# Hybrid decoder step on one core: keys and values loaded every second turn, the page chain a slot later, gate products between long chunks, low parts on VectorE

## What is computed

```python
n = rms_norm(x, g_mix)
q, k, v, xr, gr, gates = jnp.split(n @ w_in, SPLITS, axis=-1)
attn = attend(q, k, v, sb_bias)          # stick-breaking weights: exp(log_sigmoid(z) + tail sum of log_sigmoid(-z))
xc, _ = causal_dwconv(xr, rnn_buf, w_rnn_conv, b_rnn_conv)
r = sigmoid(xc @ w_rgate); i = sigmoid(xc @ w_igate)      # block diagonal, 16 blocks of 64
a = exp(-RG_C * r * softplus(-lam)); u = sqrt(1 - a*a) * i * xc
h = scan(a, u); rnn = h * gelu(gr)
gate_a, gate_b = sigmoid(gates)
x = x + (gate_a * attn + gate_b * rnn) @ w_out
```

## Time and profile before

| | us |
|---|---|
| median of 3 runs | 2364.26 |
| lowest and highest run | 2360.05, 2374.73 |
| profiled execution | 2364.8 |
| its span, first to last instruction | 2363.1 |
| TensorE busy (matmul), share of the span | 1972.6, 83% |
| VectorE busy | 1173.9, 50% |
| ScalarE busy | 940.9, 40% |
| GpSimd busy | 327.2, 14% |

### The profile page before, as it was taken

One profiled execution on the slowest core, in us unless ns is written; L12 is line 12 of the kernel. 1 busy time (PEld: TensorE's weight loads), 2 busy tenths in 40 slices (PEclk: granted clock), 3 DMA queues, 4 the chain that ended last, 5 costly groups with the idle time before them and its releaser, 6 DMA issues. The chain is left out here.

```text
span 2363.1 us, 41678 instructions
## 1 busy us (share of the span) xinstructions
PE 1972.6 (83%) x14580; PEld 1789.8 (76%) x14580; DVE 1173.9 (50%) x1987; ACT 940.9 (40%) x1514; POOL 327.2 (14%) x150
## 2 busy tenths in 40 slices
PE   4996967968687696967968779699999999999986
PEld 3896857757576584856757558699999999999985
DVE  6101535537365463635637453355555565455555
ACT  4112546655565665546655631222112222122213
POOL 4121100000000000000000120222112221122210
PEclk9998988979889797988979789799999999999998
DMA  3333222122221213222122222111111111111104
GB/s 116 97 92 84 70 61 63 44 70 59 78 66 39 70 48 79 63 62 64 44 70 59 64 96 86 53 54 42 33 50 44 46 52 36 36 52 45 44 18 159
DMA packets 206432, 148.21 MB, mean 63 GB/s; under 512 B 66485, under 2 KB 194550, under 8 KB 206228
## 3 DMA queue, kind: packets, MB, share of 16 engines
q1 hardware_dynamic: 206254, 145.99, 21.3%
HBM read 128.57 MB, written 17.61 MB: 62 GB/s over the span
## 5 line engine op out<-in xcount | busy, mean ns | idle before, releaser
L87 PE MATMUL d_p_up<-n_hi,d_w_hi 128*128 128x350 f32 x1056 | 343.7, 326 | 14.0 <-POOL d_w_lo L1613 7.7
L87 PE MATMUL d_p_up<-n_lo,d_w_hi 128*128 128x350 f32 x1056 | 342.8, 325 | 0.0
L87 PE MATMUL d_p_up<-n_hi,d_w_lo 128*128 128x350 f32 x1056 | 342.6, 324 | 0.0
L1760 DVE TENSOR_TENSOR mix<-mix,d_p_down 128x350 f32<-128x350 f32 x264 | 137.2, 520 | 320.9 <-PE d_p_down L1807 320.9
L87 PE MATMUL b_p_proj<-n_hi,b_w_hi 128*128 128x350 f32 x768 | 279.9, 364 | 0.0
L1657 ACT ACTIVATE d_up<-d_p_up 128x350 f32<-128x350 f32 x132 | 60.7, 461 | 499.8 <-PE d_p_up L87 499.8
L87 PE MATMUL b_p_proj<-n_lo,b_w_hi 128*128 128x350 f32 x768 | 258.0, 336 | 0.0
L87 PE MATMUL b_p_proj<-n_hi,b_w_lo 128*128 128x350 f32 x768 | 257.0, 335 | 0.0
L918 ACT ACTIVATE b_sums<-b_p_z,b_bias 128x720 f32<-128x720 f32 (+16 forms) x136 | 94.8, 697 | 379.9 <-PE b_p_z L1189 353.4
L1009 DVE COPY mix<-b_p_misc 128x64 f32 (+2 forms) x136 | 29.8, 219 | 420.3 <-PE b_p_misc L1220 417.9
L875 POOL TENSOR_TENSOR b_w_lo<-w_raw,b_w_hi 128x1024 fp32r<-128x1024 f32 x33 | 78.9, 2392 | 1012.2 <-ACT b_w_hi L891 1012.2
(11 more groups left out here) (248 smaller groups left out, 4066.1 us busy)
## 6 DMA issues: line engine op xcount, KB each, us to landing
w_raw<-in_w_in SPq DMA_DIRECT2D x45, 512.0 KB, 4.1
w_raw<-in_w_up SPq DMA_DIRECT2D x45, 512.0 KB, 3.8
b_page<-in_cache_k SPq DMA_DIRECT2D x128, 128.0 KB, 2.1
b_page<-in_cache_v SPq DMA_DIRECT2D x128, 128.0 KB, 2.1
w_raw<-in_w_down SPq DMA_DIRECT2D x22, 512.0 KB, 3.2
b_q_in<-q_scr SPq DMA_DIRECT2D x272, 32.0 KB, 2.3
q_scr<-a_q_stage SPq DMA_DIRECT2D x16, 260.0 KB, 3.3
b_k_in<-k_scr SPq DMA_DIRECT2D x16, 260.0 KB, 3.7
```

What stands on the lines that cost most here:

```text
L87: last = pe.matmul(out, w[:, k, :], x[:, k, col:col + CW], start=(k == 0 and w is w_hi and x is x_hi), stop=(k == KT - 1 and w is w_lo))
L1760: dve.tensor_tensor(to, to, p_down[:, n % 4, 0:CW], ALU.add).then_inc(down_out, 1)
```

## The change

Keys and values are loaded only in the first of two turns that share them; in the other, SP raises the semaphores by what the loads would have added. SP's loop runs over groups with two turns in its body. The first two query loads of a turn and its keys are issued ahead of the last two page loads of the turn before, and the values ahead of slot 3's page load. The key pages are transposed in slots 1 to 8 and multiplied in slots 2 to 9, the steps after them move by a slot, the value pages are multiplied in slots 14 to 16 and in slot 0 of the next turn, and the heads are picked in slot 3. The first gate product is made after the second gr chunk, and after it one stands between each two long chunks. The last step of the convolution moves from slot 11 to slot 9. The low parts are formed by VectorE, behind its transposed weights of the slot, and the fourth weight tile moves from slot 12 to 13.

```diff
-CHUNK_ORDER = [(w, c) for w in ("xr", "ga", "gr") for c in range(CHUNKS)] + \
-    [("rg", 0), ("gb", 0), ("ig", 0), ("rg", 1), ("gb", 1), ("ig", 1), ("rg", 2), ("gb", 2), ("ig", 2)]
+CHUNK_ORDER = [(w, c) for w in ("xr", "ga") for c in range(CHUNKS)] + \
+    [("gr", 0), ("gr", 1), ("rg", 0), ("gr", 2), ("rg", 1), ("gb", 0), ("rg", 2), ("gb", 1), ("ig", 0), ("gb", 2),
+     ("ig", 1), ("ig", 2)]
...
-W_AT = (1, 4, 8, 12)
-V_STEPS = {13: (0, 1), 14: (2, 3), 15: (4, 5), 16: (6, 7)}
-PAGES_AT = {**{s: (s + 2,) for s in range(8)}, 13: (10, 11), 14: (12, 13), 15: (14, 15)}
+W_AT = (1, 4, 8, 13)
+V_STEPS = {14: (0, 1), 15: (2, 3), 16: (4, 5), 17: (6, 7)}
+PAGES_AT = {**{s + 1: (s + 2,) for s in range(8)}, 14: (10, 11), 15: (12, 13)}
...
-                with sp.Fori(0, KT, 1) as i:
-                    group = i // 2
-                    load_q(i, 0)
-                    load_q(i, 1)
-                    load_pages(i, 0)
-                    load_pages(i, 1)
-                    sp.wait_ge(qk_done, nth(i, SLOTS, SLOTS - 1))
...
+                def first_loads(i, group, fresh):
+                    load_q(i, 0)
+                    load_q(i, 1)
+                    if fresh:
+                        sp.wait_ge(qk_done, nth(i, SLOTS, SLOTS - 1))
+                        sp.sem_inc(passed, 1)
+                        load_k(group)
+                    else:
+                        sp.sem_inc(k_arr, 32)
+
+                def turn_loads(i, group, fresh):
                     load_q(i, 2)
                     load_q(i, 3)
                     load_w(1, nth(i, 4, 1), i * P + GA_COL)
                     sp.wait_ge(inits, 6)
+                    load_w(0, nth(i, 4, 2), i * P + GR_COL)
+                    load_pages(i, 0)
+                    load_pages(i, 1)
                     sp.wait_ge(proj_done, nth(i, CHUNK_NS, CHUNK_NS - 1))
...
                     for s in range(SLOTS - 1):
                         if s + Q_RING < SLOTS - 1:
                             load_q(i, s + Q_RING)
                         if s == SLOTS - 3:
                             load_q(i, SLOTS - 1)
+                        if s == LAG and fresh:
+                            sp.wait_ge(av_group, nth(i, GROUPS, GROUPS - 1))
+                            sp.sem_inc(passed, 1)
+                            load_v(group)
+                        elif s == LAG:
+                            sp.sem_inc(v_arr, 64)
                         for j in PAGES_AT.get(s, ()):
                             load_pages(i, j)
...
+                def group_loads(group, last):
+                    turn_loads(group * 2, group, True)
+                    first_loads(group * 2 + 1, group, False)
+                    last_pages(group * 2)
+                    turn_loads(group * 2 + 1, group, False)
+                    if not last:
+                        first_loads(group * 2 + 2, group + 1, True)
+                    last_pages(group * 2 + 1)
+
+                first_loads(0, 0, True)
+                with sp.Fori(0, KVH - 1, 1) as group:
+                    group_loads(group, False)
+                group_loads(KVH - 1, True)
...
-                low_part(0, 1)
-                with pool.Fori(0, KT, 1) as i:
-                    for t in range(4):
-                        low_part((t + 1) % 2, nth(i, 4, t + 1))
...
-                        if 1 <= s <= 8:
-                            act.wait_ge(page_used, nth(i, 16, s - 1, 2))
+                        if 2 <= s <= 9:
+                            act.wait_ge(page_used, nth(i, 16, s - 2, 2))
...
-                        if s == 10:
+                        if s == 11:
                             act.wait_ge(zd_read, nth(i, 1, 0))
                             own.step(act.activation(softd[:, :, :], zd[:, :, :], ACT.Abs))
...
-                    if s in (7, 8, 11):
-                        j = {7: 2, 8: 1, 11: 0}[s]
+                    if s in (7, 8, 9):
+                        j = 9 - s
...
                         for n in range(2, groups):
                             turn_out(i, v, n)
+                        if s in W_AT:
+                            low_part((W_AT.index(s) + 1) % 2, nth(i, 4, W_AT.index(s) + 1))
                         decode(i, s)
...
-                    if s == 1 and not first:
+                    if s == 3 and not first:
                         pick_heads(i)
...
+                    if not first and s + SLOTS in V_STEPS:
+                        decode_values(i - 1, s + SLOTS)
+                    if s in V_STEPS:
+                        decode_values(i, s)
```

More of the change, by code:

```diff
@@ L567, in spread @@
         here, at = pieces[at:until], until
-        assert all(n < GATE_FIRST for n, _, _ in here) or s >= 12
+        assert all(n < GATE_FIRST for n, _, _ in here) or s >= 10
         place = []
@@ L854, in _, with last_pages @@
                             load_w(0, nth(i, 4, 4), i * P + (XR_COL + P))
+                def last_pages(i):
+                    for j in (14, 15):
+                        load_pages(i, j)
+                def group_loads(group, last):
[10 more added lines that the diff above has]
+                group_loads(KVH - 1, True)
                 for k in (1, 0):
@@ L939, in slots @@
                             high_part((t + 1) % 2, nth(i, CHUNK_NS, CHUNK_NS - 1) if t == 0
[L940 removed]
+                                      else nth(i, CHUNK_NS, TILE_LAST[t - 1], CHUNK_NS), 16 * (nth(i, 2, (0, 1, 1, 2)[t])))
                         if s == 0 and not first:
@@ L992, in _, with low_part @@
                                     g.ident[32 * n:32 * (n + 1), 32 * n:32 * n + HEADS]).then_inc(masks, 1)
+                def low_part(slot, index):
+                    dve.wait_ge(w_hi_ready, index)
+                    dve.tensor_tensor(w_lo[:, slot, :, :], w_raw[:, slot, :, :],
+                                      w_hi[:, slot, :, :].bitcast(F32), ALU.subtract).then_inc(w_lo_ready, 1)
+                low_part(0, 1)
                 def turn_out(i, s, n):
@@ L1112, in slots @@
                             values_out(i, v - 1)
-                        if s == 0 and not first:
+                        if s == 1 and not first:
                             decode_sum_out(i)
-                        if s == 2 and not first:
+                        if s == 4 and not first:
                             decode_values_out(i)
-                        if s == 9:
+                        if s == 10:
                             decode_scores_out(i)
@@ L1214, in values @@
                         pe.wait_ge(av_out, nth(i, SLOTS, s))
-                    if n == 0 and s == 6:
+                    if n == 0 and s == 7:
                         pe.wait_ge(zd_read, nth(i, 1, 0))
@@ L1233, in pick_heads, with decode_values @@
                     last.then_inc(vd_picked, 1)
[L1235 to L1268 removed]
+                def decode_values(i, s):
+                    for j in V_STEPS[s]:
                         if j == 0:
@@ L1276, in decode @@
                         last.then_inc(page_used, 1)
+                def decode(i, s, first):
+                    if 2 <= s <= 9 and (not first or s > LAG):
+                        pe.wait_ge(av_out, nth(i, SLOTS, s - LAG - 1, 1))
+                    if s == 3 and not first:
+                        pick_heads(i)
+                    if s == 4:
+                        pe.wait_ge(att_out, nth(i, 1, 0))
+                    if 2 <= s <= 9:
+                        j = s - 2
+                        pe.wait_ge(kt_out, nth(i, 8, j))
+                        for n in range(2):
+                            for pair in range(2):
+                                last = pe.matmul(p_zd[:, 8 * pair:8 * (pair + 1), 2 * j + n], k_t[:, 2 * n + pair, :],
+                                                 g.q_block[:, pair, bass.ds(i, 1), :].rearrange("p a h -> p (a h)"),
+                                                 start=True, stop=True)
+                        last.then_inc(zd_done, 1)
+                    if 1 <= s <= 8:
+                        j = s - 1
+                        pe.wait_ge(page_arr[j % 2], 32 * nth(i, 8, j // 2))
+                        if s == 1:
+                            pe.wait_ge(vd_copied, nth(i, 1, 0))
+                        for n in range(2):
+                            for pair in range(2):
+                                r = 2 * n + pair
+                                last = pe.transpose(p_kt[:, P * r:P * (r + 1)],
+                                                    page[:, j % 2, n, P * pair:P * (pair + 1)], g.ident[:, :])
+                        last.then_inc(page_used, 1)
+                    if s == 12:
+                        pe.wait_ge(laterd_done, nth(i, 1, 0))
+                        pe.matmul(p_td, g.tri[:, :], spd[:, :, 0:PAGES], start=True, stop=False)
+                        pe.matmul(p_td, g.ones[:, :], laterd[:, :, 0:PAGES], start=False, stop=True)\
+                          .then_inc(td_done, 1)
```

(4 more changed lines are left out.)

70 lines of the change are left out of this document (18 added, 52 removed).

## The result

The changed kernel takes 2277.39 us, median of 4 runs (2274.87 to 2281.52); the kernel before 2362.16, median of 4 runs (2354.39 to 2374.73), among them the three known before. The ratio is 0.9638, with a 95% interval of 0.9592 to 0.9684. A second set of 4 runs of the same kernel gave 2279.52 and 0.9633 [0.9603, 0.9663]. The forecast was 2272, 2205 to 2330.

A forecast was written before the change was run, and what follows sets the result against it. TensorE, held by others in the mixing phase (waits for keys, values and gate products, then a low clock), sets the end. Terms -82 - 24 + 3 + 10 - 52 + 35 + 15, tail +2, give -93: 2272 us, range 2205 to 2330.

The forecast's parts named there:

- Keys first, every second turn: Turn starts: key waits fall from 97 to 20 us over seven turn changes, turn 0 gains about 5; -82 us.
- in odd turns nothing else is needed: Start of odd turns: no keys to load, the query lands early, so TensorE waits about 1 us.
- the odd turns still wait long (queue): Turn starts: sign that the prediction is wrong, long waits in odd turns caused by the load queue.
- rival (3): Key and value loads land no earlier than 4 us after the forecast times, held by page waits: 2329 us, chance 0.07.
- Page chain a slot later: Slots 0 and 1: page work moves into ScalarE's burst, -21 us; moved work now in the open, +10 us.
- Values first: Slot 4: value waits of 41.5 us nearly vanish, -39, and the low clock behind them, -13; -52 us in all.
- Gate products between long chunks: Slots 10 to 16: new bank waits 65 us against 42 now, plus 12 for low clock: +35, bounds -10 and +70.
- Rival (1): The costs of new gate order and VectorE low parts are hidden, near nothing: 2222 us, chance 0.22.
- Rival (2): The costs of gate order and low parts are twice as large, each pause lowering the clock: 2322 us, chance 0.20.
- Rival (4): Slots 10 to 16: frequent pauses hold the clock at 1.2 GHz throughout, slower than before: 2420 us, chance 0.04.
- Low parts by VectorE: Slot 6: transposed weights come late, a TensorE wait of 2.1 us in seven turns: +15 us, bounds 0 and 30.
- the collision: GpSimd low part slowing a VectorE operation beside it: up to 1.4 us each, 46 us if all 33 collided; counted nothing.

The follow-up runs named there:

- experiment 1: Changed kernel with TensorE's loop written out for two turns, so it goes round ahead of turns 4 and 6 only: 2253.58 us, ratio 0.9499 to the kernel before.
- experiment 8: Changed kernel with the whole page chain a slot earlier again, decode functions back in slot 10: 2313.11 us, ratio 0.9753 to the kernel before.
- experiment 4: Changed kernel with the chunk order of the kernel before, all nine long chunks ahead of the gates' nine: 2222.60 us, ratio 0.9377 to the kernel before.
- experiment 5: Changed kernel with the old chunk order and the convolution's last step back in slot 11: 2253.34 us, ratio 0.9513 to the kernel before.
- experiment 7: Changed kernel with the low parts of the weights computed by GpSimd again: 2282.22 us, ratio 0.9625 to the kernel before.

## Why the prediction held, and where its steps did not

**The total** was right (2277 against 2272), and so was the direction of every term. That it was so near is luck: two wrong sizes cancel.

**Keys first, every second turn: -63, not -82.** The even turns wait 6.3 to 7.4 us against the 5.4 forecast, and the phase's start gained 5.7, about as forecast. What failed is the sentence "in odd turns nothing else is needed": after turn 1, which waits 0.9, they wait 5.5 to 6.4 us, not 1. TensorE's own loop went round in the kernel before too, beside the key wait of 14 us (two instruction packets of q8 lie in its gap from 904.0 to 917.4), where nothing showed it; how long it took there no run shows. The forecast named "the odd turns still wait long (queue)" as what would make it wrong; they do, but it is not the queue of SP (experiment 1). Its rival (3), loads that land 4 us late, is out: where only the keys count (experiment 1) the even turns wait 6.2 to 7.2 us, 1 to 2 more than forecast.

**Page chain a slot later: -23 and +16, forecast -21 and +10.** Mechanism and size of the gain are as forecast. Of the 7 us a turn that were to stand ahead of slot 2's scores, about half does (23.5 us in seven turns, on ScalarE's copy of scores); the other half stands ahead of slot 1's transposes (22.4 us), put down to VectorE, which the forecast did not name. The moved work cost 2.3 us a turn, within its bounds of 0 and 3. The decode functions' move out of slot 10 was worth more than the 1.2 us of their length: beside the new order the whole step is worth 34 to 36 us (experiment 8), where the forecast had 11 here and some 10 in the part on the gates.

**Values first: -46, not -52.** Turns 1 to 7 gained 6.6 us each, almost exactly the forecast. Turn 0 gained nothing: it still waits 4.7 us for its values, since its slots 0 to 3 are short (20 us instead of 36): SP issues the values from 240.19 to 242.31, and slot 4 begins at 239.2. The forecast took all eight turns alike.

**Gate products between long chunks: +15 in the table, forecast +35.** The new waits are where it put them, 2.4, 1.8, 0.6 and 2.1 us against 3.3, 1.5, 1.0 and 2.1. The experiments split the part in two. The order alone costs 55 us (experiment 4); the forecast had 65 - 26.4 + 12, about 51. The convolution's last step alone gains 31 us (experiment 5); the forecast had the wait behind it, 15.8. So the step that failed is the gain of this move: the forecast took off its wait and nothing for the low clock behind that wait, though the earlier trace rows show it (0.50). Together the two are +24 (2277.4 against 2253.3); the table's +15 compares with the kernel before, where slots 10 to 15 held other work too (41.1 us a turn, 40.4 in experiment 5). That the order's share comes out near is in part luck as well: its new waits sum to 53.5 us instead of 65, and slot 11 behind the first of them costs 2.1 us a turn more at the low clock, 17 in all, where the forecast had 12 for all slots together. One reading was wrong too: the 26.4 and 15.8 of the earlier trace rows are idle times of the weight loads (PEld). The products' own waits before sum to 31 us, not 42:

```profile
PE b_p_proj L1287 <- ACT r_gb L967: 16.6, 8, 2.1
PE b_p_proj L1287 <- issue: 14.5, 8, 1.8
```

Rival (1), both new costs hidden, names 2222 us; that the change takes 2222.6 with the old order is chance, since there the gain comes from the convolution's step. Rival (2), costs twice as large by the clock, did not come in the total. Rival (4), a clock low through all of slots 10 to 16, did not come: slot 11 is low in every turn and slot 15 in four (0.81 to 0.87), slots 12 to 14 are at 1.00.

**Low parts by VectorE: +9 in slots 5 and 6, forecast +15,** within its bounds; the wait in slot 6 is 0.5 us, not 2.1. (The forecast's own terms, 1.2 and 1.2 against 1.5 to spare, leave 0.9.) The +9 can't be put down to this move, since with GpSimd these slots are longer still. Against GpSimd the move costs nothing that shows (experiment 7), since with GpSimd slots 5 and 6, behind the collisions of slot 4, are 1.5 us a turn longer. So the step that failed is that the forecast counted the collision at nothing; in slot 4, where VectorE stood idle in the value wait, it was nothing, and this change removes that wait.

## What to carry to other kernels

Before a wait is removed, look for what lies beside it: an engine's own loop, or a neighbour that so far ran in the idle time, takes its place. A gap "for issue" with instruction packets in it is a sign of the first, and writing two turns out in the loop's body is then a cheap test. When one edit moves several things in one stretch, give each a term of its own against the kernel without it; a difference of two totals can hide a gain of 31 and a cost of 55. A wait that goes takes the low clock behind it along, so both belong in its term. On an engine that works in order, a short copy which frees a bank belongs ahead of long functions that nobody is waiting for yet.

## What the runs showed of the hardware that was not expected

Where TensorE's loop goes round and nothing else holds it, it is silent for 5.5 to 6.4 us here, with two instruction packets of 16 KB in the gap; a turn reached without that starts in 0.5 to 1.0 us. A VectorE operation of 272 columns took 2.67 us beside a GpSimd subtraction of 2.40 and 0.43 alone. In turn 4 a pause of 2.4 us in slot 10 was followed by a slot with a granted clock of 0.72 on average, that is, partly at the level of 1.2 instead of 2.4 GHz; with a pause of 0.3 us it was 1.00 and the slot 4.7 us long instead of 6.2.
